# Gate products of the RG-LRU branch as stacked hi and lo halves, with gate a inside the second unit

## The chip, the cores and the metric

One core of a Trainium2 chip runs the whole program. The time is device time in microseconds (us), taken over several runs of the same program; a median is given. A profile of one further execution gives the rows. TensorE (PE) multiplies matrices, with its weight loads shown as an engine of their own (PEld); VectorE (DVE) and ScalarE (ACT) work element by element on 128 partitions; GpSimd (POOL) does little here, and SyncE (SP) issues the weight loads.

## The reference

The kernel computes one layer of a hybrid decoder for 16 meta tokens, 1024 prompt tokens and 8 single new tokens of other sequences. Cut to what matters:

```
xn = rmsnorm(x, g1);  z = xn @ w_in
rg_x, rg_y, q, k, v, g_lr, g_out, m_a, m_b = split(z)
xc = conv4(rg_x)                                  # causal, depthwise
r  = sigmoid(blockdiag(wa) xc + ba)               # 16 blocks of 64 x 64
i  = sigmoid(blockdiag(wx) xc + bx)
log_a = -8 r softplus(-lam);  a = exp(log_a)
h_t = a_t h_(t-1) + sqrt(1 - a_t^2) (i_t xc_t)    # RG-LRU scan
ya = (h * gelu(rg_y)) @ w_branch_a
alpha = exp(log_sigmoid(g_lr @ w_gate + b) / 16)  # GLA, 4 heads, chunks of 64
o, S = gla(q, k, v, alpha)
yb = (rms(o) * g * silu(g_out)) @ w_branch_b
x  = x + (sigmoid(m_a) ya + sigmoid(m_b) yb) @ w_out
x  = x + (gelu(conv3(u_gate)) * conv3(u_val)) @ w_ffn_down
```

## The kernel before

Activations lie transposed: a feature on each of 128 partitions and C = 1050 columns (16 meta, 1024 prompt, 8 sample tokens and 2 of padding). Every weight matrix is cut into 152 units of 128 output rows by 1024 inputs. A unit is loaded to one of two slots by SP's queue, split by ACT into w_hi (`w_high`, L795, a copy rounded to fp32r) and by DVE into w_lo = raw - hi (`w_low`, L1196), and multiplied by PE in `unit` (L421): 8 k-tiles, each of three column thirds by three products (hi by hi, hi by lo, lo by hi). Two accumulators, acc[0] and acc[1], each three PSUM banks wide, take turns.

All orders are written out by hand, one per engine, and semaphores join them. The program goes through q, k and v (units 1 to 16), then the loop that the change touches, then the gate of the GLA output (`U_GO`), the branch, output and FFN matrices.

The loop (`pe.Fori` at L613) runs 8 times, j = 0 to 7. One iteration of PE is unit U_RG into acc[1] (rg_x, thirds of 350 columns), unit U_RG+1 into acc[0] (rg_y, thirds of 346), and small pieces of the GLA branch for the next 128 tokens, each placed behind a k-tile: zg (the logits of alpha, 32 rows high, L621) behind k = 2 of the first unit; keT, A, the two O pairs, and the state updates dS of bank sb6 (behind k = 6) and sb7 (behind k = 7) in the second unit. Behind the second unit stand gate a (`gate_product`, L604 to L610), onorm (sums of squares of o, L547), and gate b. A gate is three fp32 products of a block-diagonal 128 x 128 weight with a third of xc; gate a gives r's argument, gate b i's.

ACT's order in an iteration (`rg_body`, L979): first the exponentials and logarithms of the previous iteration's scan and of alpha; copies of small PSUM banks; the first conv tap with bias (xc, L995); the split of unit U_RG+2; the two squares of o (L895); then, with another table of functions, gelu of rg_y (L1005), the split of unit U_RG+3, tanh of gate a (L1009), tanh for the decay (L1013), tanh of gate b (L1017); then a table load back (L1018) and the logarithm and exponential that turn onorm into 1/rms (L901, L905). PE's zg waits for that logarithm (olog_done), since zg writes bank sb6, which holds the sums.

DVE's order (`rg_body`, L1415): o scaled by 1/rms (L1344), logits, running sums and the tail of the previous scan (L1406, L1413), evacuation of U_RG (L1224), the masked scores (L1317), three conv taps and the sample column (L1443, L1445), the split of U_RG+2 (L1196), two copies of o from PSUM (L1323), the state (L1330), the evacuation of U_RG+1 (L1224), the split of U_RG+3.

Of the kernel before, what the change touches and what calls it, by code (L numbers as in the profile page):

```python
# [112 lines left out]
def build(nc, I, O):  # L113
    ctx = ExitStack()
    with ctx:  # L115
# [31 lines left out]
        xc = nxt("rg_xc_h", C)  # L147
        rt = nxt("rg_r", C)
# [20 lines left out]
        gw = nxt("rg_gate_weights", 2 * P)  # L169
# [11 lines left out]
        gbz = nxt("gla_bias", H)  # L181
        sqk = nxt("smp_qk", 8 * NS)
# [21 lines left out]
        sq1 = (rt, it, av, th)  # L204

# [58 lines left out]
        def squares(w):  # L264
# [41 lines left out]
                             "a2_ready", "w_ready", "ml_done", "m_ready"))  # L306
        ix_ready, b_ready, h_step, ha_ready, ha_stored = (
# [103 lines left out]
        def _(pe):  # L411
# [192 lines left out]
            def gate_product(g, n_grp, half):  # L604

                pe.wait_ge(acc_free[g], n_grp)
                for n in range(3):
                    mm = nc.tensor.matmul(accv[g][:, n], gw[:, half * P:(half + 1) * P], xc[:, n * NW:(n + 1) * NW],
                                          start=True, stop=True)
                mm.then_inc(gate_mm, 1)  # L610


            with pe.Fori(0, NPAIR) as j:  # L613
# [11 lines left out]
                def O_pair(hh, bank):  # L625
# [7 lines left out]

                unit(U_RG, nth(U_RG, 2, j), 1, G_RG[1] + 2 * j, XH, XL, {
# [4 lines left out]
                    3: [lambda: O_pair(0, sb6)], 4: [lambda: O_pair(1, sb7)],  # L639
                    6: [lambda: dS_piece(sb6, n, PAIR, 0)], 7: [lambda: dS_piece(sb7, n, PAIR, 1)]})  # L640
                pe.wait_ge(xc_step, 4 * j + 4)
                pe.wait_ge(gwt_loaded, 16 * j + 16)
                gate_product(1, G_RG[1] + 2 * j + 1, 0)
                pe.wait_ge(S_ready, 2 * n + 1)
                onorm_piece(n, PAIR)
                gate_product(0, G_RG[0] + 2 * j + 1, 1)
# [132 lines left out]
        def _(act):  # L779
# [111 lines left out]

            def o_square(n, w, c0, hh):
                plain()
                act.wait_ge(o_copied, 2 * n + hh + 1)
                nc.scalar.activation(zg[:, 4 * w * hh:4 * w * (hh + 1)].rearrange("p (k t) -> p k t", k=4),  # L895
                                     V3[:, 4 * hh:4 * hh + 4, bass.ds(c0, w)], ACT.Square).then_inc(o_squared, 1)
# [81 lines left out]
            def rg_body(j, first, last):  # L978
# [29 lines left out]
                act.wait_ge(gate_mm, 2 * j + 1)  # L1008
                nc.scalar.activation(view3(rt), accv[1], ACT.Tanh, scale=0.5, bias=col(der, j)).then_inc(acc_free[1], 1)  # L1009
                plain()  # L1010
# [169 lines left out]
        def _(dve):  # L1180
# [234 lines left out]
            def rg_body(j, first):  # L1415
# [365 lines left out]
```

## Time and profile before

| | |
|---|---|
| median of 3 runs | 1923.0 us (1921.45 to 1923.09) |
| the profiled execution | 1920.77 us, its span 1919.0 us |
| PE busy | 1890.9 us (99%), 11866 products |
| DVE busy | 921.1 us (48%) |
| ACT busy | 565.7 us (29%) |
| POOL busy | 27.6 us (1%) |
| PE's granted clock, mean | 0.996 of full |
| loop of the change (8 iterations) | about 219 to 526 us of the span |

PE is busy almost throughout, so an operation added to PE, or a wait put before it, lengthens the span unless something else is taken off PE. The busy time of DVE and ACT is spread over the span; in the loop both are busier than the table says, and there the order of their work decides whether PE waits. A record of a product begins when its columns start to stream and lasts until a modelled end, so consecutive records overlap; the distance between two starts is what a product costs PE. "x6" counts records drawn together in one row; an fp32 product is recorded as two.

### The profile page before, as it was taken

Reading aid. Unit: us, or ns where it says so; the run is one execution under the profiler, and the core shown is the slowest. Engines: PE = TensorE matmul, PEld = TensorE weight load, DVE = VectorE, ACT = ScalarE, POOL = GpSimd, SP = SyncE. Lnnn points to the kernel's source line nnn. Section 1 sums busy time; section 2 is a strip of 40 time slices with the busy share of each in tenths; the row PEclk is TensorE's granted clock in tenths of the full one; section 3 lists DMA queues with packets and bytes.
Section 4 is the critical chain, followed back from the end, with each engine's and each line's share of the span. In section 5 each row is a group of like instructions: output and inputs, shape, how many; then the busy total and the mean of one; then the engine's idle time right before and its main releaser. Section 6 shows DMA issues by size and latency. Waiting matters only on the chain. (4 is left out here: it accounts for less than half of the span.)

```text
span 1919.0 us, 28820 instructions
## 1 busy us (share of the span) xinstructions
PE 1890.9 (99%) x11866; PEld 1860.3 (97%) x11866; DVE 921.1 (48%) x1067; ACT 565.7 (29%) x630; POOL 27.6 (1%) x24
## 2 busy tenths in 40 slices
PE   7999999999999999999999999999999999999998
PEld 6999899999999999999999999999999999999997
DVE  6221377788754222422244455545453545455455
ACT  5010256755642111211132332222121212131225
POOL 0000000000000000000000000000000000000032
PEclk9999999999999999999999999999999999999999
DMA  5221132223111111311131111111111111111112
GB/s 196 97 76 52 37 110 104 93 79 134 63 61 44 55 44 44 133 44 47 51 133 44 56 45 46 53 45 45 45 45 44 55 45 45 44 44 50 44 58 89
DMA packets 48234, 126.72 MB, mean 66 GB/s; under 512 B 7000, under 2 KB 20184, under 8 KB 48144
## 3 DMA queue, kind: packets, MB, share of 16 engines
q1 hardware_dynamic: 27808, 87.97, 13.6%
q10 hardware_dynamic: 20352, 37.64, 5.6%
q8 instruction: 62, 1.02, 0.2%
q14 instruction: 12, 0.10, 0.0%
HBM read 107.71 MB, written 18.14 MB: 66 GB/s over the span
## 5 line engine op out<-in xcount | busy, mean ns | idle before, releaser
L417 PE MATMUL acc<-xn_hi,w_hi 128*128 128x346 f32 (+1 forms) x2496 | 814.6, 326 | 2.5 <-issue 2.2
L417 PE MATMUL acc<-xn_lo,w_hi 128*128 128x346 f32 (+1 forms) x2496 | 803.6, 322 | 0.0
L417 PE MATMUL acc<-xn_hi,w_lo 128*128 128x346 f32 (+1 forms) x2496 | 801.5, 321 | 0.0
L417 PEld LDWEIGHTS acc<-xn_hi,w_hi 128*128 128x128 f32 x2496 | 470.9, 189 | 6.2 <-issue 3.4
L417 PEld LDWEIGHTS acc<-xn_lo,w_hi 128*128 128x128 f32 x2496 | 472.4, 189 | 1.5
L417 PEld LDWEIGHTS acc<-xn_hi,w_lo 128*128 128x128 f32 x2496 | 471.0, 189 | 0.0
L795 ACT ACTIVATE w_hi<-w_raw 128x1024 fp32r<-128x1024 f32 x149 | 156.4, 1050 | 460.2 <-PE acc L417 459.1
L1196 DVE TENSOR_TENSOR w_lo<-w_raw,w_hi 128x1024 fp32r<-128x1024 f32 x149 | 182.4, 1224 | 182.0 <-ACT w_hi L795 181.9
L417 PE MATMUL acc<-act_hi,w_hi 128*128 128x344 f32 x504 | 161.7, 321 | 2.6 <-DVE residual L1610 2.6
L417 PE MATMUL acc<-act_hi,w_lo 128*128 128x344 f32 x504 | 161.6, 321 | 0.0
L417 PE MATMUL acc<-act_lo,w_hi 128*128 128x344 f32 x504 | 161.6, 321 | 0.0
L1610 DVE TENSOR_TENSOR residual<-acc,residual 128x1032 f32<-128x1032 f32 x56 | 68.9, 1231 | 99.2 <-PE acc L417 99.2
L417 PEld LDWEIGHTS acc<-act_hi,w_hi 128*128 128x128 f32 x504 | 95.3, 189 | 4.6 <-DVE residual L1610 4.6
L417 PEld LDWEIGHTS acc<-act_lo,w_hi 128*128 128x128 f32 x504 | 95.1, 189 | 0.0
L417 PEld LDWEIGHTS acc<-act_hi,w_lo 128*128 128x128 f32 x504 | 94.8, 188 | 0.0
L1224 DVE TENSOR_TENSOR tmp<-acc,rms 128x1038 f32<-128x1038 f32 x24 | 29.7, 1239 | 134.8 <-PE acc L417 134.7
L1576 DVE TENSOR_TENSOR val_ext<-acc,rms 128x1038 f32<-128x1038 f32 x24 | 29.7, 1239 | 82.3 <-PE acc L417 82.3
L1115 ACT ACTIVATE gate_conv<-gate_ext,ffn_params 128x1032 f32<-128x1032 f32 x24 | 30.0, 1250 | 127.7 <-DVE gate_ext L1576 127.7
L1128 ACT ACTIVATE act_hi<-tmp 128x1032 fp32r<-128x1032 f32 x24 | 25.6, 1069 | 135.0 <-DVE tmp L1595 135.0
L1576 DVE TENSOR_TENSOR gate_ext<-acc,rms 128x1038 f32<-128x1038 f32 x24 | 29.7, 1239 | 72.2 <-PE acc L417 63.2
L1581 DVE SCALAR_TENSOR_TENSOR gate_conv<-gate_ext,ffn_params,gate_conv 128x1024 f32<-128x1024 f32 x48 | 61.5, 1282 | 2.9 <-DVE gate_conv L1581 0.9
L1581 DVE SCALAR_TENSOR_TENSOR tmp<-val_ext,ffn_params,tmp 128x1024 f32<-128x1024 f32 x48 | 61.5, 1282 | 2.8 <-DVE tmp L1581 0.2
(229 smaller groups left out, 2209.2 us busy)
## 6 DMA issues: line engine op xcount, KB each, us to landing
w_raw<-in_w SPq DMA_DIRECT2D x152, 512.0 KB, 3.5
ha_scratch<-rg_gelu_ha ACTq DMA_DIRECT2D x8, 519.0 KB, 2.7
h<-ha_scratch ACTq DMA_DIRECT2D x8, 519.0 KB, 6.1
residual<-in_x ACTq DMA_DIRECT2D x8, 519.0 KB, 6.4
gla_qk_pair<-qk_scratch ACTq DMA_DIRECT2D x8, 512.0 KB, 4.5
smp_v_rows<-smp_v_scratch ACTq DMA_DIRECT2D x8, 512.0 KB, 5.7
out_gla_sample<-smp_state ACTq DMA_DIRECT2D x8, 512.0 KB, 3.1
smp_state<-in_gla_state ACTq DMA_DIRECT2D x7, 512.0 KB, 4.9
```

The lines of the kernel that those rows point to most:

```text
L417: mm = nc.tensor.matmul(acc[g][:, n, 0:cw], w[s][:, t * P:(t + 1) * P], x[:, c0 + n * cw:c0 + (n + 1) * cw], start=a, stop=z)
L795: nc.scalar.activation(whi[s], raw[s], ACT.Copy).then_inc(w_hi_done[s], 1)
L1115: nc.scalar.activation(cg[:, down_c], eg[:, 2 + D0:2 + D1], ACT.Identity, scale=fpr[:, bass.ds(2 * UB + F, 1)], bias=fpr[:, bass.ds(3 * UB ...
L1128: nc.scalar.activation(blkd(AH, half * GRP + f), act_t[:, down_c], ACT.Copy).then_inc(acth_done, 1)
L1196: nc.vector.tensor_tensor(wlo[s], raw[s], whi[s].bitcast(F32), ALU.subtract).then_inc(w_split[s], 1)
L1224: nc.vector.tensor_tensor(view3(out), acc[g][0:n_part, :, 0:cw], view3(rms[0:n_part, c0:c0 + 3 * cw]), ALU.mult)\
L1576: nc.vector.tensor_tensor(view3(e_t[:, 2 + L0:2 + L1]), accl[g], view3(rms[:, late]), ALU.mult).then_inc(acc_free[g], 1)
L1581: nc.vector.scalar_tensor_tensor(c_t[:, D0:NT], e_t[:, D0 + t:t + NT], fpr[:, bass.ds(t * UB + off_b + F, 1)], c_t[:, D0:NT], ALU.mult, AL ...
L1610: nc.vector.tensor_tensor(view3(blkd(X2, m)), accd[g], view3(blkd(X2, m)), ALU.add).then_inc(acc_free[g], 1)
```

## The change

The fp32 gate products become stacked fp32r products. The host packs, for each 128 features, [wa of block 0 | wx of block 0] and [wx of block 1 | wa of block 1], and stores the pair on both halves of the partitions. On the chip gwh is its fp32r copy (ACT) and gwl = gw - gwh (DVE). Two new tiles hold xc's split: xsa = [hi of rows 0 to 63; lo of rows 0 to 63], xsb = [lo of rows 64 to 127; hi of rows 64 to 127], each made by one ACT copy and one DVE subtraction of 64 rows. Gate a takes, for each third, a 128-row product of gwh with xsa (hi by hi and hi by lo at once) and a 64-row product of gwl with the hi half; gate b the same with xsb. Each gate now holds r of one block in one half and i in the other, so r and i each come from two tanh of 64 partitions, one per gate.

Gate a moves from behind the second unit to behind its k = 6 and dS(sb6); the O pairs move one k-tile later. On ACT the copies of o come over from DVE, and the two tanh of gate a stand ahead of the gelu. On DVE the masked scores go ahead of the evacuation of U_RG, and the three subtractions stand ahead of the split of U_RG+2.

```diff
@@ -202,6 +206,7 @@
+        xsa, xsb = at("xc_hi_lo", rt_at + 2 * xc_size, C, F32R), at("xc_lo_hi", rt_at + 3 * xc_size, C, F32R)
@@ -601,12 +608,13 @@
                                               sqk[:, bass.ds(h * NS + j, 1)], start=True, stop=True)
                 mm.then_inc(so_mm, 1)
 
-            def gate_product(g, n_grp, half):
+            def gate_product(g, n_grp, xs, half, c0):
 
                 pe.wait_ge(acc_free[g], n_grp)
                 for n in range(3):
-                    mm = nc.tensor.matmul(accv[g][:, n], gw[:, half * P:(half + 1) * P], xc[:, n * NW:(n + 1) * NW],
-                                          start=True, stop=True)
+                    c = slice(n * NW, (n + 1) * NW)
+                    nc.tensor.matmul(accv[g][:, n], gwh[:, c0:c0 + P], xs[:, c], start=True, stop=False)
+                    mm = nc.tensor.matmul(accv[g][:, n], gwl[half, c0:c0 + P], xs[half, c], start=False, stop=True)
                 mm.then_inc(gate_mm, 1)
@@ -631,19 +639,22 @@
                         pe.wait_ge(keT_ready, n + 1)
                     O_piece(bank, PAIR, hh, True)
 
+                def gates_a():
+                    pe.wait_ge(gw_split, j + 1)
+                    pe.wait_ge(xs_split, 2 * j + 1)
+                    gate_product(1, G_RG[1] + 2 * j + 1, xsa, slice(0, HP), 0)
+
                 unit(U_RG, nth(U_RG, 2, j), 1, G_RG[1] + 2 * j, XH, XL, {
                     0: [lambda: vT_piece(n, PAIR, 0)], 2: [zg_pair], 3: [lambda: vT_piece(n, PAIR, 1)],
                     6: [lambda: smp_o(j)]}, cols=FULL)
                 unit(U_RG + 1, nth(U_RG + 1, 2, j), 0, G_RG[0] + 2 * j, XH, XL, {
                     1: [lambda: keT_piece(n, PAIR, so_ready, j + 1), lambda: A_piece(n, PAIR, z_ready, zn + 1)],
-                    3: [lambda: O_pair(0, sb6)], 4: [lambda: O_pair(1, sb7)],
-                    6: [lambda: dS_piece(sb6, n, PAIR, 0)], 7: [lambda: dS_piece(sb7, n, PAIR, 1)]})
-                pe.wait_ge(xc_step, 4 * j + 4)
-                pe.wait_ge(gwt_loaded, 16 * j + 16)
-                gate_product(1, G_RG[1] + 2 * j + 1, 0)
+                    4: [lambda: O_pair(0, sb6)], 5: [lambda: O_pair(1, sb7)],
+                    6: [lambda: dS_piece(sb6, n, PAIR, 0), gates_a], 7: [lambda: dS_piece(sb7, n, PAIR, 1)]})
                 pe.wait_ge(S_ready, 2 * n + 1)
                 onorm_piece(n, PAIR)
-                gate_product(0, G_RG[0] + 2 * j + 1, 1)
+                pe.wait_ge(xs_split, 2 * j + 2)
+                gate_product(0, G_RG[0] + 2 * j + 1, xsb, slice(HP, P), P)
 
             def onorm_samples():
@@ -889,6 +900,11 @@
                 act.wait_ge(keT_mm, n + 1)
                 nc.scalar.activation(bc[0:w, :], sb7[0:w, :], ACT.Copy).then_inc(keT_ready, 1)
 
+            def o_copy(n, w, c0, hh, bank):
+                plain()
+                act.wait_ge(O_mm, 2 * n + hh + 1)
+                nc.scalar.activation(V3[:, 4 * hh:4 * hh + 4, bass.ds(c0, w)], hd(bank, 4, w), ACT.Copy).then_inc(o_copied, 1)
+
             def o_square(n, w, c0, hh):
                 plain()
                 act.wait_ge(o_copied, 2 * n + hh + 1)
@@ -995,26 +1011,38 @@
                 nc.scalar.activation(xc, ext[:, 3:3 + C], ACT.Identity, scale=par("w3", j), bias=par("b", j))\
                     .then_inc(xbias_ready, 1)
                 w_high(U_RG + 2, 2, j)
+                act.wait_ge(gwt_loaded, 16 * j + 16)
+                nc.scalar.activation(gwh, gw, ACT.Copy).then_inc(gw_hi_done, 1)
                 act.wait_ge(sS_ready, j + 1)
                 act.dma_start(O["gla_sample"][j], sS).then_inc(sS_stored, 16)
                 if not last:
                     rg_prefetch(j)
+                o_copy(n, PAIR, NMETA + PAIR * j, 0, sb6)
+                act.wait_ge(xc_step, 4 * j + 4)
+                nc.scalar.activation(xsa[0:HP], xc[0:HP], ACT.Copy).then_inc(xs_hi_done, 1)
+                o_copy(n, PAIR, NMETA + PAIR * j, 1, sb7)
+                nc.scalar.activation(xsb[HP:P], xc[HP:P], ACT.Copy).then_inc(xs_hi_done, 1)
                 o_square(n, PAIR, NMETA + PAIR * j, 0)
                 o_square(n, PAIR, NMETA + PAIR * j, 1)
+                plain()
+                act.wait_ge(gate_mm, 2 * j + 1)
+                act.wait_ge(h_step, 4 * j)
+                nc.scalar.activation(view3(rt[0:HP]), accv[1][0:HP], ACT.Tanh, scale=0.5, bias=der[0:HP, bass.ds(j, 1)])
+                nc.scalar.activation(view3(it[0:HP]), accv[1][HP:P], ACT.Tanh, scale=0.5, bias=der[HP:P, bass.ds(j + KB, 1)])\
+                    .then_inc(acc_free[1], 1)
                 act.wait_ge(acc_free[0], G_RG[0] + 2 * j + 1)
                 nc.scalar.activation(gy[:, late], gy[:, late], ACT.Gelu_apprx_tanh).then_inc(gelu_ready, 1)
                 w_high(U_RG + 3, 2, j)
                 plain()
-                act.wait_ge(gate_mm, 2 * j + 1)
-                nc.scalar.activation(view3(rt), accv[1], ACT.Tanh, scale=0.5, bias=col(der, j)).then_inc(acc_free[1], 1)
-                plain()
+                act.wait_ge(gate_mm, 2 * j + 2)
+                nc.scalar.activation(view3(rt[HP:P]), accv[0][HP:P], ACT.Tanh, scale=0.5, bias=der[HP:P, bass.ds(j, 1)])\
+                    .then_inc(r_ready, 1)
+                nc.scalar.activation(view3(it[HP:P]), accv[0][0:HP], ACT.Tanh, scale=0.5, bias=der[0:HP, bass.ds(j + KB, 1)])\
+                    .then_inc(acc_free[0], 1)
+                act.wait_ge(r_ready, j + 1)
                 act.wait_ge(acc_free[1], G_RG[1] + 2 * j + 2)
                 act.wait_ge(b_ready, j)
                 nc.scalar.activation(th, rt, ACT.Tanh, scale=col(der, j + 4 * KB), bias=col(der, j + 4 * KB)).then_inc(th_ready, 1)
-                plain()
-                act.wait_ge(gate_mm, 2 * j + 2)
-                act.wait_ge(h_step, 4 * j)
-                nc.scalar.activation(view3(it), accv[0], ACT.Tanh, scale=0.5, bias=col(der, j + KB)).then_inc(acc_free[0], 1)
                 act.preload_act_table_set(LN_EXP)
                 o_rms(n, qd, PAIR, None if last else lambda: v_tokens(n + 1, PAIR, 0))
@@ -1429,12 +1457,12 @@
                 nc.vector.tensor_copy(V3[:, :, bass.ds(NT + j, 1)], hd(sb7, 8, 1)).then_inc(so_ready, 1)
                 if not first:
                     rg_tail_h(j - 1)
+                scores(n, PAIR)
+                if not first:
                     dve.wait_ge(xc_step, 4 * j)
                     dve.wait_ge(rgo_kept, j)
                     dve.wait_ge(xbias_ready, j)
                 evacuate(U_RG, 2, j, 1, ext[:, 3:3 + C])
-                scores(n, PAIR)
-                c0 = NMETA + PAIR * j
 
                 dve.wait_ge(xbias_ready, j + 1)
                 dve.wait_ge(acc_free[1], G_RG[1] + 2 * j + 1)
@@ -1445,9 +1473,13 @@
                 nc.vector.scalar_tensor_tensor(xc[:, NT:C], ext[:, NT + 3:C + 3], par("w3", j), col(rgp, j, NS, NS),
                                                ALU.mult, ALU.add).then_inc(xc_step, 1)
                 nc.vector.tensor_copy(col(rgo, j, RGW, RGW), ext[:, C + 3 - RGW:C + 3]).then_inc(rgo_kept, 1)
+                dve.wait_ge(gw_hi_done, j + 1)
+                nc.vector.tensor_tensor(gwl, gw, gwh.bitcast(F32), ALU.subtract).then_inc(gw_split, 1)
+                dve.wait_ge(xs_hi_done, 2 * j + 1)
+                nc.vector.tensor_tensor(xsa[HP:P], xc[0:HP], xsa[0:HP].bitcast(F32), ALU.subtract).then_inc(xs_split, 1)
+                dve.wait_ge(xs_hi_done, 2 * j + 2)
+                nc.vector.tensor_tensor(xsb[0:HP], xc[HP:P], xsb[HP:P].bitcast(F32), ALU.subtract).then_inc(xs_split, 1)
                 w_low(U_RG + 2, 2, j)
-                o_copy(n, PAIR, c0, 0, sb6)
-                o_copy(n, PAIR, c0, 1, sb7)
                 state(n, PAIR, 0, sb6)
                 dve.wait_ge(o_squared, 2 * n + 2)
                 sum_halves(n, PAIR)
@@ -1723,13 +1755,11 @@
-    gates = np.zeros((KB, P, 2, P), f32)
-        gates[:, 0:64, c, 0:64] = w[:, 0]
-        gates[:, 64:128, c, 64:128] = w[:, 1]
+    wa, wx = (a[n][0].reshape(KB, 2, HP, HP) for n in ("rg_wa", "rg_wx"))
+    pairs = np.stack([np.concatenate([wa[:, 0], wx[:, 0]], axis=2), np.concatenate([wx[:, 1], wa[:, 1]], axis=2)], axis=2)
+    gates = np.ascontiguousarray(np.concatenate([pairs, pairs], axis=1))
```

The order on PE, before, from the second state update of the first iteration (dS into bank small7) to gate b: rg_gate_weights is gw, rg_xc_h is xc.

```order
L540 MATMUL small7<-gla_v_tokens_71,gla_bc_keT_67 128x256
L641 REGISTER_ALU
L642 ISA [waits xc_step]
L608 MATMUL acc1<-rg_xc_h_60,rg_gate_weights_79 128x350 [waits acc_free1,gwt_loaded]
L608 MATMUL acc1<-rg_xc_h_60,rg_gate_weights_79 128x350 x2
L547 MATMUL small6<-gla_z_g_osq_66,ones_97 128x512 [waits o_summed,S_ready]
L606 REGISTER_ALU
L608 MATMUL acc0<-rg_xc_h_60,rg_gate_weights_79 128x350 [waits acc_free0]
L608 MATMUL acc0<-rg_xc_h_60,rg_gate_weights_79 128x350 x2
```

The order on PE, after, from the last product of dS into small6, through gate a, and from dS into small7 to gate b: xc_hi_lo is xsa, xc_lo_hi is xsb, rg_gate_weights_hi and _lo are gwh and gwl.

```order
L547 MATMUL small6<-gla_v_tokens_71,gla_bc_keT_67 128x256
L644 REGISTER_ALU [waits gw_split]
L616 MATMUL acc1<-xc_hi_lo_116,rg_gate_weights_hi_92 128x350 [waits acc_free1,xs_split]
L617 MATMUL acc1<-xc_hi_lo_116,rg_gate_weights_lo_80 128x350
...
L547 MATMUL small7<-gla_v_tokens_71,gla_bc_keT_67 128x256
L554 MATMUL small6<-gla_z_g_osq_66,ones_99 128x512 [waits o_summed,S_ready]
L613 REGISTER_ALU [waits xs_split]
L616 MATMUL acc0<-xc_lo_hi_117,rg_gate_weights_hi_92 128x350 [waits acc_free0]
L617 MATMUL acc0<-xc_lo_hi_117,rg_gate_weights_lo_80 128x350
```

Gate a has moved ahead of the last k-tile of the second unit and of dS into small7; it waits for the splits of gw and of xsa, and gate b for that of xsb.

The order on ACT, before, in the first iteration from the squares of o to the logarithm of onorm (rg_r is r, rg_i_b is i, rg_mult the decay's tanh, gla_qd the logarithm).

```order
L895 ACTIVATE gla_z_g_osq_66<-v_o_52 128x512 [waits o_copied,ones_done] x2
L1005 ACT_TABLE_LOAD
L1005 ACTIVATE rg_gelu_ha_65<-rg_gelu_ha_65 128x1038 [waits acc_free0]
L795 ACTIVATE w_hi0_55<-w_raw0_53 128x1024 [waits unit_done0,w_loaded0]
L1009 ACTIVATE rg_r_61<-acc1,rg_derived_89 128x1050 [waits gate_mm,ones_done]
L1013 ACTIVATE rg_mult_64<-rg_r_61,rg_derived_89 128x1050 [waits b_ready,acc_free1,ones_done]
L1017 ACTIVATE rg_i_b_62<-acc0,rg_derived_89 128x1050 [waits h_step,gate_mm,ones_done]
L1018 ACT_TABLE_LOAD
L901 ACTIVATE gla_qd_70<-small6,consts_98 128x512 [waits onorm_mm]
```

The same place on ACT after the change.

```order
L911 ACTIVATE gla_z_g_osq_66<-v_o_52 128x512 [waits o_copied,ones_done] x2
L1030 ACT_TABLE_LOAD [waits h_step,gate_mm]
L1030 ACTIVATE rg_r_61<-acc1,rg_derived_90 64x1050 [waits ones_done]
L1031 ACTIVATE rg_i_b_62<-acc1,rg_derived_90 64x1050
L1034 ACT_TABLE_LOAD
L1034 ACTIVATE rg_gelu_ha_65<-rg_gelu_ha_65 128x1038 [waits acc_free0]
L806 ACTIVATE w_hi0_55<-w_raw0_53 128x1024 [waits unit_done0,w_loaded0]
L1038 ACTIVATE rg_r_61<-acc0,rg_derived_90 64x1050 [waits gate_mm,ones_done]
L1040 ACTIVATE rg_i_b_62<-acc0,rg_derived_90 64x1050
L1045 ACTIVATE rg_mult_64<-rg_r_61,rg_derived_90 128x1050 [waits b_ready,acc_free1,r_ready]
L1046 ACT_TABLE_LOAD
L917 ACTIVATE gla_qd_70<-small6,consts_100 128x512 [waits onorm_mm]
```

The wait for gate a (gate_mm), a table load and two tanh of 64 partitions now stand ahead of the gelu, and the gelu has a table load of its own: three loads in an iteration where there were two.

The order on DVE, before and then after, from the sample column of the conv to the state.

```order
L1445 SCALAR_TENSOR_TENSOR rg_xc_h_60<-rg_ext_59,params_96,rg_smp_conv_87 128x10
L1447 ISA
L1447 COPY rg_last_columns_94<-rg_ext_59 128x13
L1196 TENSOR_TENSOR w_lo1_58<-w_raw1_54,w_hi1_56 128x1024 [waits w_hi_done1]
L1322 REGISTER_ALU [waits ones_done]
L1323 ISA [waits O_mm]
L1323 COPY v_o_52<-small6 128x4x128
L1323 ISA [waits O_mm,ones_done]
L1323 COPY v_o_52<-small7 128x4x128
L1330 SCALAR_TENSOR_TENSOR gla_state_74<-gla_state_74,gla_exp_bc_68,small6 128x256 [waits dS_mm]
```

```order
L1473 SCALAR_TENSOR_TENSOR rg_xc_h_60<-rg_ext_59,params_98,rg_smp_conv_88 128x10
L1475 ISA
L1475 COPY rg_last_columns_96<-rg_ext_59 128x13
L1477 TENSOR_TENSOR rg_gate_weights_lo_80<-rg_gate_weights_79,rg_gate_weights_hi_92 128x256 [waits gw_hi_done]
L1478 REGISTER_ALU
L1479 TENSOR_TENSOR xc_hi_lo_116<-rg_xc_h_60,xc_hi_lo_116 64x1050 [waits xs_hi_done]
L1481 TENSOR_TENSOR xc_lo_hi_117<-rg_xc_h_60,xc_lo_hi_117 64x1050 [waits xs_hi_done]
L1224 TENSOR_TENSOR w_lo1_58<-w_raw1_54,w_hi1_56 128x1024 [waits w_hi_done1]
L1355 REGISTER_ALU
L1358 SCALAR_TENSOR_TENSOR gla_state_74<-gla_state_74,gla_exp_bc_68,small6 128x256 [waits dS_mm]
```

Three subtractions have come in ahead of the split of U_RG+2 (w_lo1), each waiting for a copy of ACT, and the two copies of o have gone to ACT, where they stand ahead of the squares with the copies that make the hi halves.

## Rows read from the trace of the kernel before

**Rows 1.** Windows: stretch, length, busy us of each engine, PEclk, DMA share, GB/s.

```profile
300.00:400.00 100.00, 100.00 (x652) 94.93 (x651) 79.83 (x113) 63.04 (x76) 0.00 (x0) 1.00 0.27 94
```

**Rows 2.** Timeline of PE (start, us, line, operation): zg, first and last iteration.

```profile
227.07 0.37 PE L621 MATMUL small<-gla_low_rank,gla_gate_weights 32*128 x1
...
492.81 0.37 PE L621 MATMUL small<-gla_low_rank,gla_gate_weights 32*128 x1
```

**Rows 3.** Timeline of PE, end of the iteration of j = 2.

```profile
330.87 1.02 PE L540 MATMUL small<-gla_v_tokens,gla_bc_keT 128*128 128x256 f32 x4
331.73 1.93 PE L608 MATMUL acc<-rg_xc_h,rg_gate_weights 128*128 128x350 f32 x6
333.50 1.02 PE L547 MATMUL small<-gla_z_g_osq,ones 128*128 128x512 f32 x2
334.35 1.93 PE L608 MATMUL acc<-rg_xc_h,rg_gate_weights 128*128 128x350 f32 x6
...
336.29 0.32 PE L417 MATMUL acc<-xn_lo,w_hi 128*128 128x350 f32 x1
336.45 0.32 PE L417 MATMUL acc<-xn_hi,w_lo 128*128 128x350 f32 x1
```

**Rows 4.** Timeline of PE around zg, whose products are 32 rows high.

```profile
340.72 0.32 PE L417 MATMUL acc<-xn_hi,w_lo 128*128 128x350 f32 x1
340.97 0.48 PE L621 MATMUL small<-gla_low_rank,gla_gate_weights 32*128 x2
...
341.63 0.38 PE L621 MATMUL small<-gla_low_rank,gla_gate_weights 32*128 x2
...
342.05 0.42 PE L417 MATMUL acc<-xn_hi,w_hi 128*128 128x350 f32 x1
342.32 0.32 PE L417 MATMUL acc<-xn_lo,w_hi 128*128 128x350 f32 x1
```

**Rows 5.** Timeline of ACT, end of the same iteration; in brackets idle time before.

```profile
332.41 1.07 ACT L1005 ACTIVATE rg_gelu_ha<-rg_gelu_ha 128x1038 f32<-128x1038 f32 x1 [1.45 <-DVE rg_gelu_ha L1224]
333.38 1.04 ACT L795 ACTIVATE w_hi<-w_raw 128x1024 fp32r<-128x1024 f32 x1
334.33 1.12 ACT L1009 ACTIVATE rg_r<-acc,rg_derived 128x1050 f32<-128x1050 f32 x1
335.62 1.27 ACT L1013 ACTIVATE rg_mult<-rg_r,rg_derived 128x1050 f32<-128x1050 f32 x1 [0.18 <-issue]
336.80 1.12 ACT L1017 ACTIVATE rg_i_b<-acc,rg_derived 128x1050 f32<-128x1050 f32 x1
337.94 1.28 ACT L1018 ACT_TABLE_LOAD   x1
339.23 0.69 ACT L901 ACTIVATE gla_qd<-small,consts 128x512 f32<-128x512 f32 x1
```

**Rows 6.** Timeline of DVE after that: o's scaling, and the conv's last step.

```profile
341.21 1.23 DVE L1344 TENSOR_TENSOR v_o<-v_o,gla_qd 128x1024 f32 x1 [2.65 <-ACT gla_qd L905]
...
360.02 1.30 DVE L1443 SCALAR_TENSOR_TENSOR rg_xc_h<-rg_ext,params,rg_xc_h 128x1040 f32<-128x1040 f32 x1 [1.74 <-ACT rg_xc_h L995]
...
364.13 0.22 DVE L1445 SCALAR_TENSOR_TENSOR rg_xc_h<-rg_ext,params,rg_smp_conv 128x10 f32<-128x10 f32 x1
```

**Rows 7.** An ACT operation on 32 partitions (ns: least, median, most).

```profile
L830 ACT ACTIVATE gla_low_rank<-acc x1: 1039/1039/1039, 24.1 to 24.1; 32x1050 f32<-32x1050 f32 x1
```

**Rows 8.** Timelines of DVE and ACT behind the loop.

```profile
532.76 1.25 DVE L1394 SCALAR_TENSOR_TENSOR rg_mult<-rg_r,rg_mult 128x1050 f32<-128x1050 f32 x1
...
548.18 1.23 DVE L1196 TENSOR_TENSOR w_lo<-w_raw,w_hi 128x1024 fp32r<-128x1024 f32 x1 [3.91 <-ACT w_hi L795]
...
535.30 1.16 ACT L963 ACTIVATE rg_mult<-rg_mult,consts 128x1050 f32<-128x1050 f32 x1
```

**Rows 9.** Windows at the loop's start (columns as before).

```profile
210.00:220.00 10.00, 6.84 (x44) 5.37 (x45) 4.35 (x7) 5.14 (x10) 0.00 (x0) 0.92 0.17 56
220.00:230.00 10.00, 10.00 (x51) 9.58 (x50) 3.62 (x10) 1.55 (x5) 0.00 (x0) 0.73 0.16 54
```

More of the change, by code:

```diff
@@ L32 @@
 NMETA = 16
+HP = P // 2
 SEQ = 1024
@@ L147, in build @@
         xc = nxt("rg_xc_h", C)
+        rt_at, xc_size = off[0], (CB + 31) // 32 * 32
         rt = nxt("rg_r", C)
@@ L168, in build @@
         glr = nxt("gla_low_rank", C)
-        gw = nxt("rg_gate_weights", 2 * P)
+        gw_at = off[0]
+        gw, gwl = nxt("rg_gate_weights", 2 * P), at("rg_gate_weights_lo", gw_at, 2 * P, F32R)
         sS = nxt("smp_state", H * DV)
@@ L181, in build @@
         gbz = nxt("gla_bias", H)
+        gwh = nxt("rg_gate_weights_hi", 2 * P, F32R)
         sqk = nxt("smp_qk", 8 * NS)
@@ L306, in build @@
                              "a2_ready", "w_ready", "ml_done", "m_ready"))
+        gw_hi_done, gw_split, xs_hi_done, xs_split = (sem(n) for n in ("gw_hi_done", "gw_split", "xs_hi_done", "xs_split"))
+        r_ready = sem("r_ready")
         ix_ready, b_ready, h_step, ha_ready, ha_stored = (
@@ L1725 @@
     x = np.ascontiguousarray(tokens.T.reshape(KB, P, C))
-    vecs = [a["rg_conv_w"][0][i] for i in range(4)] + [a["rg_conv_b"][0], a["rg_ba"][0], a["rg_bx"][0],
+    vecs = [a["rg_conv_w"][0][i] for i in range(4)] + [a["rg_conv_b"][0], a["rg_ba"][0], a["rg_bx"][0].reshape(KB, 2, HP)[:, ::-1].reshape(-1),
             a["rg_lambda"][0], a["norm1_g"][0], a["gla_norm_g"][0].reshape(-1), a["norm2_g"][0], a["final_norm_g"]]
-    gates = np.zeros((KB, P, 2, P), f32)
-    for c, w in enumerate((a["rg_wa"][0], a["rg_wx"][0])):
-        w = w.reshape(KB, 2, 64, 64)
-        gates[:, 0:64, c, 0:64] = w[:, 0]
-        gates[:, 64:128, c, 64:128] = w[:, 1]
+    wa, wx = (a[n][0].reshape(KB, 2, HP, HP) for n in ("rg_wa", "rg_wx"))
+    pairs = np.stack([np.concatenate([wa[:, 0], wx[:, 0]], axis=2), np.concatenate([wx[:, 1], wa[:, 1]], axis=2)], axis=2)
+    gates = np.ascontiguousarray(np.concatenate([pairs, pairs], axis=1))
     t = np.arange(P)
```

## The prediction

> **What bounds the kernel now.** I read the windows first, then PE's timeline, then ACT's and DVE's at the seam between two iterations. The windows show the loop as PE's: 100 of 100 us busy, while DVE has 80 and ACT 63 [rows 1]. From the first zg to the eighth PE takes 265.74 us, seven periods of 37.96 [rows 2], and no wait stands in them. So two questions decide: what do PE's own instructions cost after the change, and is some result that PE had in time now late? The result nearest to being late is the logarithm of onorm, for which zg waits: it ends at 339.92 and zg starts at 340.97, 1.05 later [rows 4, 5]. ACT reaches it at the end of a closed queue: gelu, split, tanh, tanh, tanh, table load, logarithm, with 0.18 us of idle time from gelu on [rows 5].
>
> **PE's own work.** Before, a gate is three fp32 products, each recorded twice: 331.73 to 333.50, 1.77 us a gate, and 1.77 again for gate b, whose end is 336.13 (the next unit's second product starts at 336.29, one spacing of 0.16 after its first) [rows 3]. After, it is six fp32r products of 350 columns at 0.16 each, 0.95. That alone gives back 0.82 a gate, 13.1 us in sixteen.
>
> But three of the six have 64 rows, and stand between products of 128, so the height changes six times a gate. The trace has changes of height at zg, with 32 rows: zg starts 0.25 after the last 128-row product, not 0.16; its first pair of records lasts 0.48, a later pair 0.38; on the way out the starts are 342.05 and 342.32, 0.27 apart, not 0.16, and the first of them comes some 0.09 late [rows 4]. In and out that is about 0.19 a change. Six make 1.16, and a gate costs 2.11: PE is 0.34 a gate, 0.69 an iteration, longer than before. No row has 64 rows; the price lies between 0 (a gate of 0.95) and 0.19, and I take 0.19, since zg is the only change of height in the trace.
>
> **ACT behind gate a.** ACT now waits for gate a ahead of the gelu. From gate a's last product everything on ACT runs in a row: table load 1.29, two tanh, table load 1.29, gelu 0.97, split 0.95, two tanh, decay tanh 1.18, table load 1.29, by the distances of starts [rows 5]. Are tanh of 64 partitions shorter? An ACT operation of the same 1050 columns on 32 partitions takes 1.04 [rows 7], against 1.12 on 128, so no: four tanh are 4.5. The first load cannot run ahead, since the instruction that waits for gate_mm stands in front of it. The sum is 3.87 + 4.48 + 3.10 = 11.4. With 0.2 for the last product's fill (a gate's records last 1.93 for a spacing of 1.77 [rows 3]) and the hand-over, and 0.7 for the logarithm, zg is allowed 12.3 us after gate a's end.
>
> PE gets there sooner. Behind gate a it has one k-tile (nine products, 1.43), dS 0.86, onorm 0.85, gate b 2.11, and from gate b's end to zg as before 340.97 - 336.13 = 4.84 [rows 3, 4]: 10.1. PE waits 2.2 us at zg, in each iteration but the first, whose logarithm comes from before the loop. The gelu's evacuation and gate b are ready long before ACT reaches them and release nothing here.
>
> A rule of the Trainium skill would make ACT's leg longer. First the row: the load at 337.94 follows a tanh that ended at 337.92, lasts 1.28, and the logarithm starts at 339.23 [rows 5]; nothing but the load is lost. The Trainium skill, "ScalarE: Activation LUTs", section What ACT_TABLE_LOAD costs, gives a switch of sets about 1283 ns for the load and 1380 ns more for a drain. The trace agrees with the first figure and not with the second; by the page the added load would cost 2.66, and the forecast would be some 9.7 us higher (an estimate, 7 times 1.38 by that page). The sum goes by the row.
>
> **DVE and ACT ahead of gate a.** Gate a stood at 331.73, behind a conv that ended (an iteration earlier than the row shown) at about 326.4, so it had 5 us to spare. Now it comes 1.43 + 0.86 earlier on PE, and behind the conv stand ACT's copy of xc's upper half, 1.05, and DVE's subtraction, 1.25 (a half-height copy priced as in [rows 7], the subtraction as DVE's split, 1.23 [rows 8]), with three hand-overs some 2.6. From the logarithm's start to the conv's end the chain runs over DVE and ACT alone: 339.23 to 364.35, 25.1 us [rows 5, 6]; its waits end on ACT (2.65 for the exponential, 1.74 for the biased xc [rows 6]). So gate a may start 25.1 + 2.6 = 27.7 after the logarithm's start, 27.0 after a zg that starts 0.75 after it. PE needs from zg to gate a's new place 331.73 + 37.96 - 340.97 - 2.29 = 26.4. It waits another 0.5.
>
> A period is thus 37.96 + 0.69 + 2.2 + 0.5 = 41.4. Round the loop as a check: 25.1 + 2.6 + 2.3 (gate a with its fill) + 11.4 = 41.4. Excess 3.45.
>
> **What costs nothing.** The packed weights go in the same DMA of 128x256, at the same place of ACT's queue. ACT's copies of o and of gwh (0.6 and below), and xsb's hi half, fall into the time in which ACT waits for DVE and PE ahead of the squares. DVE loses two copies of o and gains three subtractions, some 1.5 net, ahead of the split of U_RG+2; that split is wanted by the next iteration's first product, 10 us after its old place, so the cover is the second unit's last k-tiles. The scores ahead of the evacuation wait for A, which PE has done by then. If one of these covers is gone, its price is at most its own length, 0.5 to 1.5 an iteration.
>
> **Behind the loop.** The logarithm ended 3.8 after gate b's end; now it ends 12.3 after gate a's, 7.1 after gate b's: ACT is 3.3 later against PE. The decay's logarithm had 535.30 - 534.01 = 1.3 to spare behind DVE's product [rows 8], so 2.0 goes through to the gate unit whose split at 548.18 PE already waited for. Bounds 0 and 3.3; I take 2.0.
>
> **Sum.** First iteration +0.7, seven of +3.45 make 24.2, the tail +2.0: +26.9. The profiled execution took 1920.8 (span 1919.0), so 1947.7 for one like it; the median is 2.2 above it, and 1923.0 + 26.9 gives **1950**.
>
> **The rivals.**
> - *Changing the height is free with 64 rows.* PE then saves 1.64 an iteration and waits the longer: round the loop 25.1 + 2.6 + 1.15 + 11.4 = 40.25, an excess of 2.3 in six iterations, 1.8 in the first two, and a tail of 3.1. Time 1941.7. Nothing speaks for it but that zg's 32 rows are another height; the same time, near 1941, would come if the first table load ran ahead of its wait.
> - *ACT is in time and the products pay: faster.* Its place is zg. If ACT's leg from gate a's end to the logarithm's end is under PE's 8.9 (10.1 less 1.16), no wait arises and the 13.1 us stay: 1909.9. It needs half-height tanh at half price (2.2 less), the first load hidden (1.3 less) and free changes of height, all three; the 1.04 on 32 partitions speaks against the first [rows 7].
> - *The clock falls in the waits.* Ahead of the loop, where PE was busy for 6.84 of 10 us, the granted clock then stood at 0.73 over the next ten, partly the 1.2 GHz level [rows 9]: 2.7 us of work lost. If each of the seven waits at zg did that, 19 more: 1969. The waits here are 2.2 in 41 us of full work, much less than in that stretch.
> - *The loads drain.* By that mechanism ACT loses another 1.4 at the added load in seven iterations, 1959.6. The load at 337.94 shows none [rows 5].
> - *All of it is hidden*, about 1923: every wait would have to be mis-sized at once.
>
> **How the numbers follow.** Forecast 0.66, free changes or a hidden load 0.15, clock 0.06, draining loads 0.04, faster 0.06, no change 0.03. The forecast's own range is 1944 to 1956: the tail's bounds and 0.5 an iteration on hand-overs and fill. With the first rival and the draining loads it reaches 1938 to 1961, holding 0.85. A difference of 0.2% is about what a measurement of this kernel tells from none; faster 0.06, within it 0.03, slower 0.91.
>
> **What would show it.** Right: zg waiting some 2 us for ACT's logarithm from the second iteration on, three table loads an iteration, tanh of 64 partitions at 1.05 to 1.12, a gate's six products at about 2.1, periods of 41.4. Wrong: a gate at 0.95 (first rival), tanh near 0.6, the first load ahead of gate a's end, or PE at 100% in the loop.

## The result, and the profile after

The changed kernel takes 1967.6 us (median of 6 runs, 1966.4 to 1973.1) where the kernel before took 1922.7: a ratio of 1.0244, interval 1.0232 to 1.0256, 45 us slower. The forecast was 1950, its range ended at 1961. The direction and the wait at zg that it named are there; one cost that it had set aside came on top.

The page of the changed kernel, from an execution that took 1973.1 us: its span, and busy time, share and instructions of each engine. The mean granted clock of TensorE in this execution is 0.983; it was 0.996.

```profile
span 1971.2 us, 28910 instructions
...
PE 1923.3 (98%) x11866; PEld 1881.6 (95%) x11866; DVE 934.8 (47%) x1075; ACT 626.8 (32%) x694; POOL 27.8 (1%) x24
```

PE now waits inside the loop. Its waits in this execution (line waited for: us in total, times, longest):

```profile
PE small L629 <- ACT gla_qd L917: 18.8, 7, 2.7
...
PE acc L424 <- DVE w_lo L1224: 1.6, 1, 1.6
```

L629 is zg and L917 the logarithm of onorm: seven waits of 2.7 us, one in each iteration but the first. The timeline of PE, at gate a of one iteration and then at zg of the first, second and last iteration:

```profile
391.78 0.42 PE L617 MATMUL acc<-xc_hi_lo,rg_gate_weights_lo 64*128 64x350 f32 x1
392.14 0.43 PE L616 MATMUL acc<-xc_hi_lo,rg_gate_weights_hi 128*128 128x350 f32 x1
392.49 0.42 PE L617 MATMUL acc<-xc_hi_lo,rg_gate_weights_lo 64*128 64x350 f32 x1
...
231.91 1.15 PE L629 MATMUL small<-gla_low_rank,gla_gate_weights 32*128 x8
...
273.32 0.57 PE L629 MATMUL small<-gla_low_rank,gla_gate_weights 32*128 x1 [2.66 <-ACT gla_qd L917]
...
539.66 0.57 PE L629 MATMUL small<-gla_low_rank,gla_gate_weights 32*128 x1 [2.69 <-ACT gla_qd L917]
```

Each product of a gate starts 0.35 to 0.36 after the one before, where an undisturbed product of 350 columns takes 0.16: six of them 2.1 us, as forecast. From the first zg to the second, 41.41 us pass, the 41.4 of the sum. But from the second to the eighth there are six periods of 44.39 (266.34 in all), and before it was 37.96 on average [rows 2]. A record of zg is 0.57 long where it was 0.37, which says what else changed: PE runs slower there. Windows around one wait (stretch, length, busy us of PE, PEld, DVE, ACT, POOL, PEclk, DMA share, GB/s):

```profile
393.50:403.80 10.30, 10.30 (x53) 8.29 (x52) 6.73 (x14) 9.95 (x9) 0.00 (x0) 1.00 0.21 60
403.80:406.50 2.70, 0.03 (x1) 0.00 (x0) 0.97 (x3) 2.67 (x4) 0.00 (x0) 0.94 0.39 159
406.50:413.00 6.50, 6.48 (x24) 6.20 (x25) 4.15 (x4) 4.93 (x8) 0.00 (x0) 0.50 0.07 20
413.00:420.00 7.00, 7.00 (x50) 7.00 (x50) 6.29 (x9) 5.10 (x7) 0.00 (x0) 1.00 0.00 0
```

PE is idle for 2.7 us, and for the 6.5 us behind it the granted clock is 0.50, 1.2 GHz in place of 2.4: half of 6.5 us of work is lost, 3.2 us, about the 3.0 by which these periods exceed 41.4. The same stands behind all seven waits; in the kernel before nothing like it stands behind the first zg, where PEclk is 1.00 [rows 1]. Not every wait of the changed kernel is followed by a fall: behind the loop PE waits 1.6 for w_lo, and in the 7 us behind that the clock stays up. That window, and the two at the loop's start (compare [rows 9]):

```profile
210.00:220.00 10.00, 7.91 (x44) 6.35 (x42) 2.61 (x3) 4.81 (x8) 0.00 (x0) 0.75 0.18 56
220.00:230.00 10.00, 8.99 (x33) 7.67 (x34) 3.08 (x9) 1.43 (x4) 0.00 (x0) 0.57 0.01 2
602.30:609.30 7.00, 7.00 (x44) 7.00 (x45) 3.71 (x4) 3.10 (x3) 0.00 (x0) 1.00 0.23 75
```

The fall at the loop's start is longer here than in the profile before (0.75 and 0.57 for 0.92 and 0.73), and the first zg starts 4.8 us later, which the sum doesn't cover. This varies by execution: in the profiles of five runs below that leave the changed kernel's order as it is up to the first zg, that zg starts between 225.6 and 232.0. The profiled execution is 5.4 us above the median of its kernel.

What fills ACT between gate a and the logarithm (start, us, line; in brackets idle time before):

```profile
393.72 1.28 ACT L1030 ACT_TABLE_LOAD   x1 [1.24 <-PE acc L617]
395.01 1.13 ACT L1030 ACTIVATE rg_r<-acc,rg_derived 64x1050 f32<-64x1050 f32 x1
396.16 1.13 ACT L1031 ACTIVATE rg_i_b<-acc,rg_derived 64x1050 f32<-64x1050 f32 x1
397.31 1.28 ACT L1034 ACT_TABLE_LOAD   x1
398.61 1.07 ACT L1034 ACTIVATE rg_gelu_ha<-rg_gelu_ha 128x1038 f32<-128x1038 f32 x1
399.58 1.05 ACT L806 ACTIVATE w_hi<-w_raw 128x1024 fp32r<-128x1024 f32 x1
400.65 1.14 ACT L1038 ACTIVATE rg_r<-acc,rg_derived 64x1050 f32<-64x1050 f32 x1
401.82 1.14 ACT L1040 ACTIVATE rg_i_b<-acc,rg_derived 64x1050 f32<-64x1050 f32 x1
402.98 1.27 ACT L1045 ACTIVATE rg_mult<-rg_r,rg_derived 128x1050 f32<-128x1050 f32 x1
404.26 1.28 ACT L1046 ACT_TABLE_LOAD   x1
405.56 0.69 ACT L917 ACTIVATE gla_qd<-small,consts 128x512 f32<-128x512 f32 x1
```

No gap stands in it: 11.84 us from the first load to the logarithm, against 11.4 in the sum. Set it beside [rows 5], where the same stretch had one load, and tanh of 128 partitions in the time that tanh of 64 takes here.

### The profile page after: what moved, and what is told of

Read it like the earlier page. It is cut to its first block and busy times, and to the rows that moved or that the text cites. A ratio compares the mean times of both kernels' runs of the same rounds, so it can differ in the third digit from the quotient of the medians.

```text
span 1971.2 us, 28910 instructions
## 1 busy us (share of the span) xinstructions
PE 1923.3 (98%) x11866; PEld 1881.6 (95%) x11866; DVE 934.8 (47%) x1075; ACT 626.8 (32%) x694; POOL 27.8 (1%) x24
```

## The experiments

Theory A: ACT's leg behind gate a makes zg wait, and that wait, whatever causes it, is what brings the clock down behind it. Rival B: the clock falls for the new products (64 rows among 128), not for the wait. Rivals C and D: gate a's new place, or the new order on ACT, costs by itself.

**Filling the wait.** Eighteen more products on PE ahead of zg; rg_x gets a k-tile twice more than it should.

```diff
+                def filler():
+                    for _ in range(2):
+                        tile_products(slot_of(U_RG), 2, 1, XH[:, 2 * C:3 * C], XL[:, 2 * C:3 * C], False, False, FULL)
-                    0: [lambda: vT_piece(n, PAIR, 0)], 2: [zg_pair], 3: [lambda: vT_piece(n, PAIR, 1)],
+                    0: [lambda: vT_piece(n, PAIR, 0)], 2: [filler, zg_pair], 3: [lambda: vT_piece(n, PAIR, 1)],
```

> The change with 18 more products (two k-tiles, 2.88 us) on PE right ahead of zg in every iteration; they add a k-tile to the first unit twice more, so rg_x is not the reference's. Theory A: PE works where it waited, zg waits for nothing or nearly, the clock stays at full in the loop, the period falls from 44.4 to 41.5 and the time to about 1954, although PE does 23 us more work. Rival B: the clock falls as before, the period stays at 44 or more, the time at 1968 or above.

Measured: 1955.1 us, 12.6 less than with the change, with 23 us more work on PE. Windows of the loop, first of this kernel and then of the change:

```profile
300.00:400.00 100.00, 100.00 (x607) 89.98 (x606) 75.89 (x112) 76.46 (x87) 0.00 (x0) 1.00 0.29 94
400.00:500.00 100.00, 100.00 (x635) 92.76 (x634) 77.20 (x108) 73.24 (x88) 0.00 (x0) 1.00 0.23 78
```

```profile
300.00:400.00 100.00, 94.62 (x537) 84.76 (x536) 71.33 (x99) 72.03 (x83) 0.00 (x0) 0.93 0.25 86
400.00:500.00 100.00, 91.93 (x527) 84.42 (x526) 71.87 (x103) 73.19 (x84) 0.00 (x0) 0.91 0.25 83
```

PE is at 100% and its clock at full, with the 64-row products in place: rival B falls. The filler puts 23.0 us of work where 18.8 us were waited, so without a change of clock the time would have risen by 4.2; it fell by 12.6. By the medians the falls of the clock cost 16.8 us of the change's time. By the two profiled executions it is somewhat more: their spans, 1971.2 and 1955.6, differ by 15.6, so 19.8, and seven periods' excess of 3.0 makes 21. The price is 17 to 21 us.

**The table ahead of the wait.** One load fewer and the first one out of ACT's leg:

```diff
+GELU_TANH = "gelu_apprx_tanh_and_others"
...
                 o_square(n, PAIR, NMETA + PAIR * j, 1)
+                act.preload_act_table_set(GELU_TANH)
                 plain()
                 act.wait_ge(gate_mm, 2 * j + 1)
```

> The change with one thing added: the table of gelu and tanh is loaded right behind the squares of o, ahead of the wait for gate a, so that tanh and gelu share one load and an iteration has two loads again. Theory A (ACT's leg behind gate a makes zg wait 2.7 us, and that wait is what halves the clock afterwards): the wait at zg shrinks to about 0.8 us (the gelu then waits for its evacuation instead), the period is near 39.9 us, and if 0.8 us no longer halves the clock the time is near 1939. Rival B (the clock falls for another reason, the 64-row products, and not for the wait): the wait shrinks as in A but the clock still falls in every iteration, period near 42 to 43, time near 1957.

Measured: 1945.8 us, ratio 1.0124 (1.0107 to 1.0141). Its wait at zg in PE's list:

```profile
PE small L630 <- ACT gla_qd L918: 7.4, 7, 1.1
```

The start of ACT's leg on the timeline:

```profile
381.38 1.14 ACT L1032 ACTIVATE rg_r<-acc,rg_derived 64x1050 f32<-64x1050 f32 x1
382.53 1.13 ACT L1033 ACTIVATE rg_i_b<-acc,rg_derived 64x1050 f32<-64x1050 f32 x1
384.21 1.07 ACT L1036 ACTIVATE rg_gelu_ha<-rg_gelu_ha 128x1038 f32<-128x1038 f32 x1 [0.55 <-DVE rg_gelu_ha L1254]
```

And windows of 7 us behind two of the waits:

```profile
392.40:399.40 7.00, 6.92 (x36) 6.74 (x37) 4.96 (x6) 6.48 (x9) 0.00 (x0) 0.76 0.05 19
433.80:440.80 7.00, 6.96 (x46) 6.83 (x47) 5.58 (x6) 6.91 (x10) 0.00 (x0) 1.00 0.08 19
```

The two loads taken out of the leg bring the wait from 2.7 to 1.1 us and the time down by 22 us, nearly half of the loss. The gelu then waits 0.55 for its evacuation, as expected. The time lies between A's 1939, for a clock that stays up, and B's 1957, for one that falls each time: it still fell behind six of the seven waits, each time for a shorter stretch than with the change (0.76 over 7 us), and not behind the fifth (1.00), which is as long. This run alone doesn't tell A from B.

**128 rows for the lo weights.**

```diff
-                    mm = nc.tensor.matmul(accv[g][:, n], gwl[half, c0:c0 + P], xs[half, c], start=False, stop=True)
+                    mm = nc.tensor.matmul(accv[g][:, n], gwl[:, c0:c0 + P], xs[:, c], start=False, stop=True)
```

> The change with the lo weights multiplied over all 128 rows (which adds the product lo by lo) in place of 64 rows: no change of row height in a gate. Theory A: a gate takes 0.95 us in place of 2.1, ACT's leg stays, zg waits at least as long (2.3 us or more), the clock still falls in seven iterations: period near 43.1, time near 1960. Rival B (64-row products bring the clock down): the clock stays full from the second iteration on and the time is near 1942. If a change of row height costs nothing, a gate stays at its time and the whole at 1968.

Measured: 1957.3 us, ratio 1.0177 (1.0160 to 1.0194). PE's timeline in gate a:

```profile
384.48 0.32 PE L617 MATMUL acc<-xc_hi_lo,rg_gate_weights_lo 128*128 128x350 f32 x1
384.64 0.33 PE L616 MATMUL acc<-xc_hi_lo,rg_gate_weights_hi 128*128 128x350 f32 x1
384.80 0.32 PE L617 MATMUL acc<-xc_hi_lo,rg_gate_weights_lo 128*128 128x350 f32 x1
```

And its wait at zg:

```profile
PE small L629 <- ACT gla_qd L917: 21.9, 7, 3.2
```

The products stand 0.16 apart, not 0.355: a change of row height costs 0.19 at 64 rows too, the price taken from zg's 32 [rows 4]. PE gains 1.16 a gate, and part of that goes to waits: zg waits 3.1 us instead of 2.7, and onorm 0.3 to 0.4. The clock is down behind each wait at zg although no 64-row product is left, so rival B's 1942 is off here too. **Both edits together:**

> Both edits: the load ahead of gate a's wait, and 128 rows for the lo weights. Theory A: zg waits 1.6 us; the period is 39.5 if that wait leaves the clock alone (time near 1934), near 42.5 if it doesn't (near 1955). Rival B: clock full, 1934, whatever the wait.

Measured: 1942.7 us, ratio 1.0109 (1.0091 to 1.0126), with waits of 1.9 at zg. The clock stayed up behind the first of the seven and fell behind the other six, so the periods go from 39.1 to 40.8; the time lies between the two that were given for A, 1934 and 1955.

**The kernel before, with the wait alone.** Two idle table loads ahead of the logarithm's:

```diff
+                act.preload_act_table_set("exp_and_others")
+                act.preload_act_table_set("sigmoid_and_others")
                 act.preload_act_table_set(LN_EXP)
```

> The kernel before, its fp32 gates and its order untouched, with two idle table loads on ACT ahead of the load of the logarithm's table, so that the logarithm of onorm comes 2.6 us later. Theory A (a wait at zg halves the clock behind it, whatever the gates are): zg waits about 1.6 us in seven iterations, and the clock falls behind each wait; the period goes from 37.96 to 40.2 by the wait alone (time near 1940) and to 41 to 42 with the clock (time near 1945 to 1952). Rival B (the fall belongs to the new products): clock full in the loop, time near 1940. If a load cost 1.4 us more than its 1.28, the wait would be above 4.

Measured: 1945.0 us, ratio 1.0120 (1.0101 to 1.0138). ACT's timeline at the end of an iteration:

```profile
428.23 1.28 ACT L1018 ACT_TABLE_LOAD   x1
429.52 1.28 ACT L1019 ACT_TABLE_LOAD   x1
430.81 1.28 ACT L1020 ACT_TABLE_LOAD   x1
432.11 0.69 ACT L901 ACTIVATE gla_qd<-small,consts 128x512 f32<-128x512 f32 x1
```

PE's wait for it:

```profile
PE small L621 <- ACT gla_qd L901: 11.9, 7, 1.7
```

And a window that begins with the end of one such wait:

```profile
433.00:436.50 3.50, 3.44 (x17) 3.33 (x18) 2.42 (x3) 3.47 (x5) 0.00 (x0) 0.72 0.14 37
```

A load costs 1.29 from start to start, three times over, and nothing behind it. The rule of the Trainium skill ("ScalarE: Activation LUTs", section What ACT_TABLE_LOAD costs) that adds a drain to each switch is not borne out here. With fp32 gates in their old place the waits bring the clock down as well, but behind five of the seven only. Behind the first two, of 1.6 and 1.7, it stayed up; the window behind the second:

```profile
308.50:315.50 7.00, 7.00 (x46) 6.86 (x47) 5.61 (x6) 6.85 (x10) 0.00 (x0) 1.00 0.06 19
```

Three periods have no fall in them: 39.6, up to the first wait, and then 40.3 and 40.4, where 40.2 was expected of the wait alone. The others are 41.3 to 42.9.

**Undoing the place, and the order on ACT.** Gate a behind the second unit again:

```diff
-                    6: [lambda: dS_piece(sb6, n, PAIR, 0), gates_a], 7: [lambda: dS_piece(sb7, n, PAIR, 1)]})
+                    6: [lambda: dS_piece(sb6, n, PAIR, 0)], 7: [lambda: dS_piece(sb7, n, PAIR, 1)]})
+                gates_a()
```

> The change with gate a back behind the second unit, all else as changed. Theory A: ACT's leg of 12.3 us starts 2.3 us of PE's work later, so zg waits longer, 3.8 us by the sum without the clock, and the time is higher than with the change, near 1985: the new place of gate a is a gain in itself. Rival C (the new place of gate a is what costs): the time falls below the change's 1967.

Measured: 1979.9 us, ratio 1.0302 (1.0283 to 1.0321). zg waits 4.1 us, and the next iteration's first product 0.7 to 0.8 for tanh of gate a. The new place makes the changed kernel 12 us faster than it would be without it, and rival C falls. Now the gelu and the split of U_RG+3 ahead of gate a's two tanh again:

```diff
+                act.wait_ge(acc_free[0], G_RG[0] + 2 * j + 1)
+                nc.scalar.activation(gy[:, late], gy[:, late], ACT.Gelu_apprx_tanh).then_inc(gelu_ready, 1)
+                w_high(U_RG + 3, 2, j)
                 plain()
                 act.wait_ge(gate_mm, 2 * j + 1)
...
-                act.wait_ge(acc_free[0], G_RG[0] + 2 * j + 1)
-                nc.scalar.activation(gy[:, late], gy[:, late], ACT.Gelu_apprx_tanh).then_inc(gelu_ready, 1)
-                w_high(U_RG + 3, 2, j)
```

> The change with the two tanh of gate a back behind the gelu and the split, so that the gelu's table serves them and there are two loads an iteration. Theory A: acc[1] is freed some 2 us late, so PE now waits about 2 us at the next iteration's first product and 0.6 at zg; without the clock the period is 41.7, as much as with the change; with the clock halved behind the 2 us wait the time is near 1968. So the order alone mends nothing. Rival D (the evacuation ahead of the gelu, not the added load, is what costs): no wait, period near 39, time near 1931.

Measured: 1956.2 us, ratio 1.0178 (1.0160 to 1.0197). Its waits on PE:

```profile
PE acc L424 <- ACT rg_i_b L1034: 16.0, 8, 2.1
...
PE small L629 <- ACT gla_qd L917: 2.3, 3, 0.8
```

The wait has moved, as A said, from zg to the next iteration's first product, which needs acc[1]; the three periods in which the clock stayed up are 41.5 to 41.6, near the sum without the clock, 41.7, and the other four 42.1 to 42.7. Rival D's 1931 is far off. A's 1968 is also too high, by 12: the clock fell behind five of these eight waits, and behind three of the same length (1.9 to 2.0) it stayed up.

**A version with neither mixed gates nor changes of height.** The gates stay in their place, and each becomes nine fp32r products of 128 rows; ACT keeps two full tanh and two loads. As in the change, ACT takes the copies of o and DVE the masked scores first; on ACT the split of U_RG+3 moves behind tanh of gate a and the decay's tanh behind that of gate b. The main cuts:

```diff
-                    mm = nc.tensor.matmul(accv[g][:, n], gw[:, half * P:(half + 1) * P], xc[:, n * NW:(n + 1) * NW],
-                                          start=True, stop=True)
+                    for w, x, a, z in ((gwh, xch, True, False), (gwh, xcl, False, False), (gwl, xch, False, True)):
+                        mm = nc.tensor.matmul(accv[g][:, n], w[:, half * P:(half + 1) * P], x[:, n * NW:(n + 1) * NW],
+                                              start=a, stop=z)
...
+                nc.scalar.activation(xch, xc, ACT.Copy).then_inc(xs_hi_done, 1)
...
                 w_low(U_RG + 2, 2, j)
-                o_copy(n, PAIR, c0, 0, sb6)
-                o_copy(n, PAIR, c0, 1, sb7)
+                dve.wait_ge(xs_hi_done, j + 1)
+                nc.vector.tensor_tensor(xcl, xc, xch.bitcast(F32), ALU.subtract).then_inc(xs_split, 1)
```

> The kernel before with its gates in place and unmixed, each as nine fp32r products of 128 rows (hi by hi, hi by lo, lo by hi) instead of three fp32 products; one ACT copy and one DVE subtraction split xc, the copies of o go to ACT and the scores go first as in the change, the split of U_RG+3 goes behind tanh of gate a and the decay's tanh behind that of gate b (its tile holds xc's lo half). A gate takes 1.44 in place of 1.77 and no height changes. Theory A: no wait arises at zg, the clock stays, the period falls from 37.96 to 37.3 and the time by 5.3 us to about 1917. Rival: ACT and DVE already bind at 38 and PE waits for what it saves: no change, 1922.

Measured: 1916.9 us, ratio to the kernel before 0.9972 (0.9962 to 0.9981): 0.3% faster, clear of the noise but small. A window of the loop:

```profile
300.00:400.00 100.00, 100.00 (x672) 97.41 (x671) 81.75 (x119) 69.98 (x87) 0.00 (x0) 1.00 0.26 91
```

PE's timeline, two products of gate b, and zg in the first and the last iteration:

```profile
336.26 0.32 PE L614 MATMUL acc<-xc_lo,rg_gate_weights_hi 128*128 128x350 f32 x1
336.42 0.32 PE L614 MATMUL acc<-xc_hi,rg_gate_weights_lo 128*128 128x350 f32 x1
...
230.37 0.37 PE L627 MATMUL small<-gla_low_rank,gla_gate_weights 32*128 x1
...
491.84 0.37 PE L627 MATMUL small<-gla_low_rank,gla_gate_weights 32*128 x1
```

Seven periods of 37.35 us, with no wait at zg and the clock at full: the 0.6 us an iteration that PE saves stay saved.

## Why the prediction was wrong, point by point

- **PE's own work**: right. A gate takes 2.1 us (0.355 a product), and by 128 rows in every product 0.95. The price read off zg's 32 rows holds at 64. The rival of free changes, 1942, had no ground. That zg is the only change of height in the trace is not so: ahead of the loop there are products of 16 rows, which the prediction didn't use.
- **ACT's leg**: right in kind, short by 0.4: 11.84 for 11.4. Tanh of 64 partitions takes 1.13 to 1.14, a little more than the 1.12 on 128, and the split and the decay's tanh come 0.1 later than before. Three loads an iteration, the first behind the wait, as forecast.
- **The waits**: right in kind. zg waits 2.66 to 2.69 in place of 2.2: from gate a's end (the next product's start, 393.55) to zg ACT's leg takes 13.0 in place of 12.3, and PE has 10.3 of work in place of 10.1. The 0.5 at gate a can't be seen in this profile, since the slow clock behind each wait delays PE by more: gate a starts 26.3 after the first zg and 29.2 after the others, when its input has been ready for 0.8. In the run with the table ahead, in the one iteration whose clock stayed up behind its wait, gate a starts 26.6 after zg, right behind its input, so it waited some 0.4 there: the 0.5 was about right, but hidden behind the fall. The first period, 41.41, has no fall and no wait at gate a, and that it equals the forecast of 41.4 is partly luck: the sum had 0.5 too little at zg, and 0.5 at gate a that isn't in this period. So is the total of the waits, 18.8 measured and 18.9 in the sum.
- **The tail**: about right. PE waits 1.6 behind the loop for the split and 0.7 for the samples' sums, where the kernel before waited 0.3 for the split: 2.0 more, the forecast's figure.
- **The clock**: wrong, and the step that failed. The prediction named it as a rival, with its place and its price (1969, against 1967.6 measured), and gave it 0.06, because "The waits here are 2.2 in 41 us of full work, much less than in that stretch" ahead of the loop. So the sum had the clock at nothing. The trace of before had one fall amid its work, at the sparse stretch [rows 9], and no wait of this length between dense work; two of 1.0 and 1.2 behind the loop left the clock at 1.00. It couldn't bear that argument for 2.2 either way. In its place the runs showed waits of 2.7 that bring the clock to 0.50 all seven times, for 17 to 21 us, and 1967.6 - 1950 is 17.6. PE's added work (eight times 0.69), the waits, the tail and the clock, 5.5 + 18.8 + 2.0 + 16.8, make 43 of the 45 us. A rival that rows neither showed nor excluded should have lain inside the range.
- **What costs nothing**: right, as far as the profile shows. PE's waits list has no other wait in the loop.

Where the expected gain of single-pass products went: the changes of height took it back (0.95 became 2.1, more than fp32's 1.77), and mixing r and i doubled the tanh on the engine whose queue ends at zg. With the heights and the first load mended, zg still waits 1.9.

## What to carry to other kernels

A step that PE waits for is priced by what ACT still has to do behind it, table loads included, and by what PE has left in the meantime; here 13.0 us against 10.3, and 12.3 against 10.1 in the sum. When PE is full, price each new wait twice, as the wait and as the slower clock behind it, and keep that case in the range. Halving the partitions of an operation saved nothing here (tanh on ACT 1.13 to 1.14 on 64 and 1.12 on 128; DVE's subtraction 1.25 on 64), and a 64-row product between full ones cost more than a product of 128 rows.

## What the runs showed of the hardware

- Waits of PE of 1.0 to 4.1 us amid dense work were followed by a stretch at half the granted clock in many iterations of seven kernels, with and without 64-row products. All 21 waits of 2.5 to 4.1 us were (the change, full rows, gate a put back). Of the shorter ones at zg some were not: of seven waits of 1.0 to 1.1 us one (PEclk 1.00 behind it, 0.76 behind another), of seven of 1.6 to 1.8 two, of seven of 1.9 one. No run here shows what decides between them.
- More work on PE made the kernel faster: 23 us more products in place of 18.8 us of waits, 12.6 us less time.
- A change of row height between 128 and 64 costs 0.19 us, as between 128 and 32. The Trainium skill ("TensorEngine Tiling (Array Packing)", section Key Properties) says that a change of tiling mode drains TensorE. The trace agrees that a change costs time, and gives the price; it doesn't show that a drain is what takes it.
- Table loads on ACT run back to back at 1.29 us each.
